# Sums of squares of q and k with the squares as the moving operand, four heads on four column blocks

## The reference, cut to what matters

```python
def l2_normalize(x):
    return x * lax.rsqrt(jnp.sum(x * x, axis=-1, keepdims=True) + L2_EPS)

qkv = jax.nn.silu(causal_dw_conv(qkv_ext, conv_gdn)).astype(f32)
q = l2_normalize(qkv[..., :GDN_QK_W].reshape(bsz, t, GDN_HEADS, GDN_DK)) * (GDN_DK ** -0.5)
k = l2_normalize(qkv[..., GDN_QK_W:2 * GDN_QK_W].reshape(bsz, t, GDN_HEADS, GDN_DK))
```

## Time and profile before

| what | value |
|---|---|
| median of 3 runs | 1414.47 us |
| lowest, highest | 1412.2, 1415.42 us |
| span of the profiled execution | 1412.4 us |
| PE busy | 1391.3 us, 99% |
| PE weight loads busy | 1369.1 us, 97% |
| DVE busy | 862.0 us, 61% |
| ACT busy | 629.7 us, 45% |
| DMA, mean rate | 135 GB/s |

### The profile page before, as it was taken

One profiled execution on the slowest core, in us unless ns is written; L12 is line 12 of the kernel. 1 busy time (PEld: TensorE's weight loads), 2 busy tenths in 40 slices (PEclk: granted clock), 3 DMA queues, 4 the chain that ended last, 5 costly groups with the idle time before them and its releaser, 6 DMA issues.

```text
span 1412.4 us, 25251 instructions
## 1 busy us (share of the span) xinstructions
PE 1391.3 (99%) x10788; PEld 1369.1 (97%) x10788; DVE 862.0 (61%) x1510; ACT 629.7 (45%) x1002; POOL 32.4 (2%) x130
## 2 busy tenths in 40 slices
PE   9999999999999999999999999999999999999997
PEld 8999999898999999999999999998999999999997
DVE  5655533787697765553376555337886968655433
ACT  5443333582644544433354333335826345444331
POOL 0000000110000000000000000001100000000000
PEclk9999999999999999999999999999999999999998
DMA  6544344422216334434435443444221263444342
GB/s 220 208 149 149 121 143 141 132 90 87 71 61 217 118 130 142 149 122 144 155 121 207 150 149 117 140 142 140 90 93 65 90 214 122 150 149 149 123 144 99
DMA packets 49760, 190.93 MB, mean 135 GB/s; under 512 B 6160, under 2 KB 8720, under 8 KB 49136
## 3 DMA queue, kind: packets, MB, share of 16 engines
q1 hardware_dynamic: 49040, 184.19, 38.9%
q0 software_dynamic: 608, 5.12, 0.9%
HBM read 182.86 MB, written 6.43 MB: 134 GB/s over the span
## 4 chain that ended last, share of the span: by engine, by line
PE 95%; DVE 3%; ACT 1%; issue 0%; DMA 0%; SPq 0%
PE PS L1493 27%; PE PS L1494 27%; PE PS L1495 27%; PE PS L1533 2%; PE PS L1664 2%; PE PS L1538 2%; PE PS L1534 2%; DVE WL L1040 1%; PE PS L1813 1%; PE PS L1662 1%; PE PS L1705 1%; ACT XH L751 1%; DVE XL L1052 1%; PE PS L1769 1%; PE PS L1788 1%; DVE X L1104 0%
## 5 line engine op out<-in xcount | busy, mean ns | idle before, releaser
L1493 PE MATMUL PS<-XH,WH 128*128 128x336 f32 (+1 forms) x1728 | 550.6, 319 | 0.0
L1495 PE MATMUL PS<-XH,WL 128*128 128x336 f32 (+1 forms) x1728 | 543.2, 314 | 0.0
L1494 PE MATMUL PS<-XL,WH 128*128 128x336 f32 (+1 forms) x1728 | 542.8, 314 | 0.0
L1040 DVE TENSOR_TENSOR WL<-RAW,WH 128x1024 fp32r<-128x1024 f32 (+1 forms) x312 | 398.8, 1302 | 193.3 <-ACT WH L734 192.8
L734 ACT ACTIVATE WH<-RAW 128x1024 fp32r<-128x1024 f32 (+1 forms) x312 | 343.1, 1118 | 222.0 <-DMA RAW<-in_w_down 173.3
L1493 PEld LDWEIGHTS PS<-XH,WH 128*128 128x128 f32 x1728 | 325.4, 188 | 1.4 <-issue 0.4
L1494 PEld LDWEIGHTS PS<-XL,WH 128*128 128x128 f32 x1728 | 325.5, 188 | 0.3
L1495 PEld LDWEIGHTS PS<-XH,WL 128*128 128x128 f32 x1728 | 325.2, 188 | 0.0
L1493 PE MATMUL PS<-HH,WH 128*128 128x336 f32 (+1 forms) x704 | 221.4, 314 | 0.0
L1494 PE MATMUL PS<-HL,WH 128*128 128x336 f32 (+1 forms) x704 | 221.3, 314 | 0.0
L1495 PE MATMUL PS<-HH,WL 128*128 128x336 f32 (+1 forms) x704 | 221.2, 314 | 0.0
(11 more groups left out here) (252 smaller groups left out, 1220.7 us busy)
## 6 DMA issues: line engine op xcount, KB each, us to landing
RAW<-in_w_up SPq DMA_DIRECT2D x176, 512.0 KB, 4.3
RAW<-in_w_down SPq DMA_DIRECT2D x64, 704.0 KB, 4.1
RAW<-in_w_in SPq DMA_DIRECT2D x56, 512.0 KB, 4.3
RAW<-in_w_out SPq DMA_DIRECT2D x16, 512.0 KB, 4.2
SEQ_S<-in_states SPq DMA_DIRECT2D x2, 2048.0 KB, 9.7
out_state_s<-SEQ_S POOLq DMA_DIRECT2D x2, 2048.0 KB, 8.9
X<-in_x SPq DMA_DIRECT2D x8, 168.0 KB, 4.8
out_y<-X SPq DMA_DIRECT2D x4, 320.0 KB, 2.3
```

Source lines behind the costliest of these rows:

```text
L1040: dve.tensor_tensor(WL[slot][:, cols], RAW[slot][:, cols], WH[slot][:, cols].bitcast(F32), ALU.subtract).then_inc(split_lo.sem, 1)
L1493: pe.matmul(out, wh, xh, start=first, stop=False)
L1494: pe.matmul(out, wh, xl, start=False, stop=False)
L1495: return pe.matmul(out, wl, xh, start=False, stop=last)
```

## The change

`sq` squares only the 336 real columns, into one of four buffers: the two `SQX` and the two `SQY` of the output norm. `sq_sum` and its semaphore are gone. In its place:

- `qk_sum` g (g = 0 for q, 1 for k) on PE waits for the fourth square of its four and makes four fp32 products. The stationary operand is 128x32 of ones, the moving one the 336 squares of a head; head h writes partitions 32h to 32h+31 of one bank. Each of the 32 rows of a block holds the same sums. ACT copies the bank (128x336) to the new buffer `SUMS`.
- `qk_col` g on PE transposes `SUMS` against the identity, three blocks of 128 tokens, into another bank; DVE adds EPS to every 32nd column of it and writes `SSQ`.

`norms` waits for its own two `qk_col` steps in place of `sq_sum`. `qk_sum` 0 stands behind part 10 ahead of `silu` 5, `qk_col` 0 behind part 11. `qk_sum` 1 stands behind part 21 after `sq` 7, followed by `qk` 2. `qk_col` 1 then stands behind part 22, ahead of `norms`, `kk` 2, `unit` 2, `qk` 0 and `kk` 0, which move there with it. The four new groups take their turns in banks 5 to 7, and later groups move on by two or four places.

```diff
-    [("gate_g",), ("silu", 1), ("sq_sum", 0), ("tap", 3)],
-    [("sq", 1), ("conv", 2), ("sq_sum", 1), ("lo", 1, 1), ("conv", 3), ("silu", 2), ("hi", 2, 1), ("tap", 4), ("sq", 2), ("hi", 3, 0),
+    [("gate_g",), ("silu", 1), ("tap", 3)],
+    [("sq", 1), ("conv", 2), ("lo", 1, 1), ("conv", 3), ("silu", 2), ("hi", 2, 1), ("tap", 4), ("sq", 2), ("hi", 3, 0),
      ("lo", 2, 0), ("conv", 4), ("hi", 3, 1), ("evac", 5)],
-    [("silu", 3), ("tap", 5), ("silu", 4), ("cum",), ("sq_sum", 2), ("lo", 2, 1), ("sq", 3), ("evac", 6)],
+    [("silu", 3), ("tap", 5), ("silu", 4), ("cum",), ("lo", 2, 1), ("sq", 3), ("evac", 6)],
     [("conv", 5)],
-    [("silu", 5)],
-    [],
+    [("qk_sum", 0), ("silu", 5)],
+    [("qk_col", 0)],
     [("evac", 7), ("gb", 2), ("lo", 3, 0), ("tap", 7)],
...
-    [("tap", 8), ("sq_sum", 3), ("sq", 5), ("conv", 7), ("lo", 4, 0), ("table",)],
-    [("conv", 8), ("sq_sum", 4), ("silu", 6), ("hi", 4, 1)],
-    [("sq_sum", 5)],
-    [("evac", 9), ("silu", 7), ("silu", 8), ("evac", 10), ("sq", 6), ("sq", 7), ("sq_sum", 6), ("sq_sum", 7), ("norms",), ("qk", 2),
-     ("kk", 2), ("unit", 2), ("qk", 0), ("kk", 0)],
-    [("lo", 4, 1)],
+    [("tap", 8), ("sq", 5), ("conv", 7), ("lo", 4, 0), ("table",)],
+    [("conv", 8), ("silu", 6), ("hi", 4, 1)],
+    [],
+    [("evac", 9), ("silu", 7), ("silu", 8), ("evac", 10), ("sq", 6), ("sq", 7), ("qk_sum", 1), ("qk", 2)],
+    [("qk_col", 1), ("norms",), ("kk", 2), ("unit", 2), ("qk", 0), ("kk", 0), ("lo", 4, 1)],
...
                         act.wait_ge(act_out.sem, silu_of("qkv", t, layer))
-                        if t >= 2:
-                            act.wait_ge(sq_summed.sem, sq_summed.at(t - 2, layer))
-                        act.activation(SQX[t % 2][:, :], QKV[:, t, :], ACT.Square).then_inc(qk_sq.sem, 1)
+                        if t >= HEADS:
+                            act.wait_ge(filled.sem, filled.at(GROUP_INDEX["qk_sum", 0], layer))
+                        act.activation(SQUARES[t % HEADS][:, 0:T], QKV[:, t, 0:T], ACT.Square).then_inc(qk_sq.sem, 1)
+                    elif what == "qk_sum":
+
+                        group(step, layer)
+                        evacuated(act.activation(SUMS[:, 0:T], row_bank(step), ACT.Copy))
...
-                        dve.wait_ge(sq_summed.sem, sq_summed.at(2 * HEADS - 1, layer))
-                        ch.step(dve.tensor_scalar(SSQ[:, :, :], QK_COLS, EPS, None, ALU.add))
-
+                        own(("qk_col", 0), layer)
+                        own(("qk_col", 1), layer)
...
+                    elif what == "qk_col":
+
+                        sums = group(step, layer)[:, 0:TT, 0:P:SQUARE]
+                        evacuated(dve.tensor_scalar(SSQ[:, :, t * HEADS:(t + 1) * HEADS], sums, EPS, None, ALU.add))
...
-                    elif what == "sq_sum":
-
-                        pe.wait_ge(qk_sq.sem, qk_sq.at(t, layer))
-                        if t == 0:
-
-                            pe.wait_ge(to_act.sem, to_act.at(0, layer))
+                    elif what == "qk_sum":
+
+                        pe.wait_ge(qk_sq.sem, qk_sq.at((t + 1) * HEADS - 1, layer))
+                        bank_free(step, layer)
+                        for h in range(HEADS):
+                            ins = pe.matmul(row_bank(step)[block(h)], mask("ones", SQUARE), SQUARES[h][:, 0:T], start=True, stop=True)
+                        ins.then_inc(filled.sem, 1)
+                    elif what == "qk_col":
+
+                        evacuated(("qk_sum", t), layer)
+                        bank_free(step, layer)
                         for q in range(TT):
-                            ins = pe.matmul(QK_COLS[:, q, t:t + 1], SQX[t % 2][:, tcols(q)], mask("ones", 1), start=True, stop=True)
-                        ins.then_inc(sq_summed.sem, 1)
+                            ins = pe.transpose(heads_bank(step)[:, q, :], SUMS[:, tcols(q)], mask("ident"))
+                        ins.then_inc(filled.sem, 1)
```

More of the change, by code:

```diff
@@ L212 @@
 EVACUATED_BY = {
-    "gate_rows": "dve", "cum": "act", "gb": "act", "qk": "dve", "kk": "dve", "vt": "act", "x": "dve", "y": "dve",
+    "gate_rows": "dve", "qk_sum": "act", "qk_col": "dve", "cum": "act", "gb": "act", "qk": "dve", "kk": "dve", "vt": "act", "x": "dve", "y": "dve",
     "yt": "dve", "kt": "act", "kst": "dve", "nv": "dve", "ks": "dve", "o": "act", "st": "dve", "rob": "dve",
@@ L305, in decoder_trunk @@
         (XM0, XM1), xm_end = stack(sq_at, ("XM0", [P, HEADS, P], F32), ("XM1", [P, HEADS, P], F32))
-        SQX = [SQX0, SQX1]
         assert xm_end <= sq_end - (TP - T) * 4
         SQY = [sb(f"SQY{i}", [P, TP]) for i in range(2)]
+        SQUARES = [SQX0, SQX1, *SQY]
         ACCX = sb("ACCX", [P, TP])
@@ L319, in decoder_trunk @@
         SSQ = sb("SSQ", [P, TT, 2 * HEADS])
+        SUMS = sb("SUMS", [P, TP])
         h_at = region(2 * FT * T * 4)
@@ L401, in decoder_trunk @@
         act_out = sig("act_out", QKV_T + 4)
-        qk_sq, sq_summed = sig("qk_sq", 2 * HEADS), sig("sq_summed", 2 * HEADS)
+        qk_sq = sig("qk_sq", 2 * HEADS)
         mix_y, mix_hi, mix_lo = sig("mix_y", 4), sig("mix_hi", 2), sig("mix_lo", 2)
@@ L449, in heads_bank, with row_bank @@
             return PS[:, 5 + GROUP_INDEX[name] % 3, :].rearrange("p (h n) -> p h n", h=HEADS)
+        def row_bank(name):
+            return flat(heads_bank(name))[:, 0:T]
         def small_mask(name):
@@ L477, in decoder_trunk @@
         SEQ_GL = CUM[:, 48:84].rearrange("p (h s) -> p h s", h=HEADS)
-        QK_COLS = PS[:, 4, 48:72].rearrange("p (t c) -> p t c", t=TT)
         O_COLS = PS[:, 4, 72:84].rearrange("p (t h) -> p t h", t=TT)
@@ L665, in _ @@
                 pool.memset(buf[:, :, T:TP].bitcast(F32), 0.0)
-            for buf in (*SQX, *SQY, ACCX):
+            for buf in (*SQY, ACCX, SUMS):
                 pool.memset(buf[:, T:TP], 0.0)
```

## The result

| | before | after |
|---|---|---|
| median of 6 runs | 1414.74 us | 1424.32 us |
| lowest, highest | 1412.2, 1416.45 us | 1421.77, 1425.75 us |
| span of the profiled execution | 1412.4 us | 1420.0 us |
| ratio, 95% interval | 1 | 1.0074 [1.0063, 1.0085] |

The changed kernel is 9.6 us slower in the medians (forecast 1425.3 us), 7.6 us in the profiled spans. The page of after, to be read beside the earlier trace rows: busy time by engine, then the shares of the chain by engine.

The account below looks back on a forecast made before the run. PE, busy 99% of the span, was taken to bound the kernel. Per layer -3.1 + 5.0 + 2.0 + 1.5 = +5.4 us, twice +10.8, on 1412.4 gives 1423.2, plus 2.1 for the median: 1425.3 us, range 1417 to 1433.

Parts of the forecast that it names:

- PE's own work: On PE, eight `sq_sum` (5.3 us) go, two `qk_sum` (0.75) and two `qk_col` (0.35) come: -3.1 us per layer.
- The wait at `qk_sum` 0: Behind part 10, PE stands until ACT ends `sq` 3: 5.0 us per layer, bounds 4.5 and 5.5.
- The wait at `qk_sum` 1: Behind part 21, PE stands until ACT ends `sq` 7: 2.0 us per layer, floor 1.0, top 3.0.
- `nt` 2: Behind part 22, `norms` makes `nt` 2 later, using 1.4 us of slack before `x` 2 2; 0 to 0.5 us, taken as nothing.
- The clock: A stretch near half clock on PE behind the long wait: 1.5 us per layer, bounds 0 and 3.0.
- Up to `x` 2 2: The per-layer sum of PE's work, both waits and the clock: -3.1 + 5.0 + 2.0 + 1.5 = +5.4 us.
- The gaps of layer 0: Rival: PE's two idle gaps at 338.5 and 349 us close, 5.1 us come back, 1420.2 us; chance 0.08.
- the sum of the spans: The profiled span of before, 1412.4 us, plus +10.8 us for both layers: 1423.2 us.
- The rival "no first wait, and faster": `sq` 3 on ACT ends before PE finishes part 10; no waits or half clock, -6.2 us, 1408.3 us; chance 0.10.

Follow-up runs that it names:

- The shifted kernels: The kernel before, and the version with both sums late, each with 158 more PE semaphore instructions in the first block: 1411.66 us (0.9987) and 1412.31 us (0.9991).
- the late order: The changed kernel with `qk_sum` 0 and 1 and their consumers moved to later places (`qk_sum` behind parts 15 and 23): 1408.11 us, 0.9962 of before.
- the second profiles of before and after: Both kernels, unchanged, run and profiled once more: 1412.6 us for before and 1422.07 us for after, one run each.

## Why the prediction was right, and where it wasn't

- **PE's own work.** `qk_sum` measured 0.70 us at full clock (taken as 0.75), `qk_col` 0.33 (0.35). The surplus over the two rounds of 0.28 us is 0.14 us, like the 0.16 of the earlier trace rows: four column blocks on the same rows run side by side as blocks with rows of their own do. But the sum counted what the matmul behind an `sq_sum` loses and not what `qk_sum` costs the matmuls on both its sides: in the stream it is 0.9 us (the kernel with `qk_sum` 0 late), so that PE's own work fell by some 2.8 us per layer and not 3.1. The estimate from the Trainium skill (TensorE: Matmul & The Clock Gate, Packing small matmuls) was 0.71 us, and the trace agrees. The drain that the Trainium skill names for a change of tiling mode (TensorEngine Tiling (Array Packing), Key Properties) can be no more here than the 0.35 us by which the group in the stream exceeds its two rounds.
- **The wait at `qk_sum` 0.** Forecast 5.0; measured 5.14 - 0.15 = 5.0 us in layer 0 and 5.2 in layer 1. It came from subtracting removed PE work on one engine's timeline from a fixed point on another's. The kernels with `sq` 3 sooner, or with less ahead of it, showed the cause twice: the wait fell by 4.1 and by 1.75 us.
- **The wait at `qk_sum` 1.** Forecast 2.0; measured 2.0 and 2.1. The arithmetic was right and its story wrong: I put it down in part to `gb` being late. With the first wait gone and `gb` on time it is 2.2 us. It is the three removed `sq_sum` (2.0 us) between `gb` 1 and this place, with ACT's `sq` 7 about as far behind `gb` 1 as before.
- **`nt` 2.** Forecast no wait. DVE ends it at 330.8 us and PE reaches `x` 2 2 at 330.9: none, as said.
- **The clock.** The step that was mis-sized: 1.5 us per layer, with 3.0 us at half clock read from gaps of 1 us. Behind 5 us of waiting the half clock lasted 4.6 us in layer 0, and kept at full clock `x` 2 2 comes 2.2 and 3.3 us sooner. Of the 3.3 in layer 1, 1.7 belong to the first wait and 1.6 to a stretch behind the second, which the forecast had named and left to its upper bound of 3.0; the measured cost is above that bound.
- **Up to `x` 2 2** the sum was +5.4 per layer and the traces have +5.9 and +6.8. The clock (0.7 and 1.8 us more than taken) and `qk_sum` (0.3 more) are at least the whole surplus.
- **The gaps of layer 0.** A rival with 0.08, taken to hang on PE's queue filling while it stands. They did close and gave 5.6 us back in the profiled execution. The shifted kernels show that another place of the instructions is enough for that, with no wait added; whether PE's standing had a part in after isn't shown. The kernel in which PE doesn't stand at `qk_sum` 0 has gaps again, but its instructions lie elsewhere too. So the sum of the spans was 3.2 us too high (1423.2 forecast, 1420.0 measured), and the median came out at 1424.3, since it lies 4.3 us above after's span, not the 2.1 I carried over. Each run of after took 1.7 to 1.8 us more than its own span, and the profiled one was the fastest of the six, 2.5 us below the median: that is the 4.3. The forecast of 1425.3 is near because these two errors and the clock's have different signs; in that it was lucky.
- **The rival "no first wait, and faster".** Its price was wrong. I had let the second wait go with the first; with no first wait (the kernel with `qk_sum` 0 late) the time is 1411.9 us and not 1408.3, no clear gain on before.

What stays open: a gap moves when instructions are added far ahead of it and ends 1.3 to 1.5 us after a packet of PE's instructions has landed, in all 16 cases; that is shown. Why some packets come in time and others don't is not. Nor is it shown what makes the clock fall behind some waits of 2 us and gaps of 1 us and not behind others.

## What to carry to other kernels

When work is taken off the bounding engine, draw the other engines' times of the steps that it meets next and subtract: what was removed between two meeting points becomes a wait at the second, unless the partner has slack. Move the meeting point with the saving, ask also for the step behind it (who reads the result, and what stands ahead of the reader), and count the clock behind any long wait. And before a gain of 0.3% is put down to an edit, compare stretch by stretch up to a common instruction, and time both kernels shifted: most of such a gain can be the place of the program's instructions.

## What the hardware showed that was not expected

- PE stood 0.4 to 1.4 us without a releaser in dense runs of small products, 16 times in 14 traces, each time until 1.3 to 1.5 us after a 16 KB packet of its instructions had landed. Nine of the 16 have a half clock behind them; it is some 5 us in one layer of before. 158 semaphore instructions of PE, added in the first block, removed two gaps and made another (layer 0 shorter by 1.2 to 2.5 us, layer 1 longer by 2.1); in the late order they cost 3.7 and 1.7 us.
- A wait of 5.0 us was followed by 4.6 us at half clock in layer 0 of after, waits of 3.1 and 3.2 us by a half clock too, waits of 0.6 to 1.5 us in the mixers by none. Of the 16 waits of 1.8 to 2.3 us in the mixers that began at full clock, five had a half clock behind them, and after has one of each kind: 1.85 us in layer 0 without, 1.95 us in layer 1 with 3.4 us at 0.50. In the second profiles of before and after the first gap had no half clock and the 1.95 us wait had it again.
- A half clock also came with no idle time of PE ahead of it: in the shifted kernel before, PE is busy 7.0 of the 7 us from 286 to 293 at full clock, and is granted 0.51 from 293 to 296. It is busy all of 365.0 to 378.4 us too, and is granted 0.50 from 378.4 to 381.8.
- Four fp32 products of 128x32 by 336 columns on four column blocks take 0.70 us together at full clock and 1.27 at half; full width and in turn they take 2.36 and 4.16 us, 3.3 to 3.4 times as much. In the stream of weight matmuls the blocks cost 0.9 us in all.
